# Four modulation pieces of a two-block model: scaled and added on ScalarE and GpSimd instead of streamed through TensorE

## What is computed

```python
cond = jax.nn.silu(c)
for i in range(DEPTH):                                  # DEPTH = 2
    mod = (cond @ ada_w[i] + ada_b[i])[:, None, :]      # 1024 -> 6 * 1024
    sh1, sc1, ga1, sh2, sc2, ga2 = jnp.split(mod, 6, axis=-1)
    u = x * (1 + sc1) + sh1
    ...                                                 # mixer
    x = _layer_norm(DEEPNORM_ALPHA * x + (1 + ga1) * y, ln_g[i, 0], ln_b[i, 0])
    u = x * (1 + sc2) + sh2
    ...                                                 # feed-forward
```

```python
def step(S, inp):
    r_t, k_t, v_t, w_t, a_t, b_t = inp
    sa = jnp.einsum('bhvk,bhk->bhv', S, a_t)
    S = S * w_t[:, :, None, :] + sa[..., None] * b_t[:, :, None, :] + v_t[..., None] * k_t[:, :, None, :]
    return S, jnp.einsum('bhvk,bhk->bhv', S, r_t)
```

## Time and profile before

| what | us |
|---|---|
| three executions | 2178.11, 2184.09, 2178.46 (median 2178.46) |
| the profiled execution | 2178.67 |
| its span | 2176.7 |
| TensorE busy | 2051.6 |
| VectorE busy | 1138.9 |
| ScalarE busy | 911.2 |
| GpSimd busy | 709.2 |

### The profile page before, as it was taken

The page is one execution under the profiler, slowest core; times in us unless marked ns, Lnnn a source line. Parts: engine busy times, 40 slices in busy tenths (PEclk is TensorE's granted clock), DMA queues, the critical chain, the costliest instruction groups (busy, mean ns, idle before and its releaser), DMA issues.

```text
span 2176.7 us, 40478 instructions
## 1 busy us (share of the span) xinstructions
PE 2051.6 (94%) x17526; PEld 1868.1 (86%) x17526; DVE 1138.9 (52%) x2177; ACT 911.2 (42%) x1331; POOL 709.2 (33%) x316
## 2 busy tenths in 40 slices
PE   3998999999999998999999999999999999999998
PEld 3786777889998887899999896799989998868897
DVE  6236645764483447654542447654264417357652
ACT  0452222544555425544333554333343336444443
POOL 0270000413683004136314560321561166313134
PEclk9998999999999999999999999999999999999999
DMA  8475334355443014554444440354445443314552
GB/s 323 190 294 222 128 134 150 142 188 194 155 173 138 3 40 155 190 181 154 176 174 175 153 157 22 126 174 175 170 146 175 175 174 136 136 48 151 190 194 78
DMA packets 49681, 340.48 MB, mean 156 GB/s; under 512 B 6368, under 2 KB 8416, under 8 KB 8672
## 3 DMA queue, kind: packets, MB, share of 16 engines
q1 hardware_dynamic: 49504, 337.90, 42.6%
HBM read 336.83 MB, written 1.05 MB: 155 GB/s over the span
## 4 chain that ended last, share of the span: by engine, by line
PE 84%; DVE 7%; ACT 3%; DMA 2%; issue 2%; POOL 1%; SPq 0%; ACTq 0%; POOLq 0%; DVEq 0%
PE bank L548 84%; DMA ada_ring<-ada 2%; POOL ring_low L2716 1%; PE bank L554 1%; DVE arena L2024 1%; DVE arena L2418 1%; DVE arena L2011 1%; DVE ZZ L2265 0%; DVE arena_parts L2047 0%; ACT high L1533 0%; DVE XX L2274 0%; DVE arena L2253 0%; POOL acc L2760 0%; ACT arena_parts L1558 0%; DVE acc L2117 0%
## 5 line engine op out<-in xcount | busy, mean ns | idle before, releaser
L548 PE MATMUL bank<-arena_parts,high 128*128 128x272 f32 (+2 forms) x4512 | 1019.2, 313 | 34.0 <-ACT arena_parts L1558 27.8
L548 PEld LDWEIGHTS bank<-arena_parts,high 128*128 128x128 f32 x4512 | 744.2, 190 | 83.6 <-issue 36.2
L548 PE MATMUL bank<-arena_parts,ring_low 128*128 128x272 f32 (+2 forms) x2736 | 778.6, 287 | 0.0
L1533 ACT ACTIVATE high<-ring 128x2048 fp32r<-128x2048 f32 x237 | 453.2, 1914 | 604.9 <-PE bank L548 589.4
L2716 POOL TENSOR_TENSOR ring_low<-ring,high 128x2048 fp32r<-128x2048 f32 x105 | 484.2, 4616 | 559.8 <-ACT high L1533 520.1
L548 PEld LDWEIGHTS bank<-arena_parts,ring_low 128*128 128x128 f32 (+1 forms) x2736 | 519.0, 190 | 1.2
L2060 DVE TENSOR_TENSOR ring_low<-ring,high 128x2048 fp32r<-128x2048 f32 x132 | 304.5, 2307 | 180.2 <-ACT high L1533 180.2
L548 PE MATMUL bank<-hidden_high,high 128*128 128x256 f32 (+1 forms) x1056 | 303.1, 287 | 0.0
L548 PE MATMUL bank<-hidden_low,high 128*128 128x256 f32 (+1 forms) x1056 | 301.0, 285 | 0.0
L548 PE MATMUL bank<-hidden_high,ring_low 128*128 128x256 f32 (+1 forms) x1056 | 300.2, 284 | 0.0
L2716 POOL TENSOR_TENSOR hidden_low<-arena,hidden_high 128x256 fp32r<-128x256 f32 (+1 forms) x132 | 111.7, 849 | 575.4 <-DVE hidden_high L2076 575.2
(11 more groups left out here) (332 smaller groups left out, 2160.5 us busy)
## 6 DMA issues: line engine op xcount, KB each, us to landing
ring<-stream SPq DMA_DIRECT2D x269, 1024.0 KB, 4.8
ada_ring<-ada SPq DMA_DIRECT2D x48, 1024.0 KB, 6.1
con<-consts SPq DMA_DIRECT2D x1, 1542.5 KB, 11.4
con<-consts SPq DMA_DIRECT2D x1, 1040.0 KB, 6.9
arena<-xin SPq DMA_DIRECT2D x1, 1024.0 KB, 11.5
out<-arena SPq DMA_DIRECT2D x2, 512.0 KB, 2.9
prob_even<-consts SPq DMA_DIRECT2D x1, 384.0 KB, 11.9
par<-params SPq DMA_DIRECT2D x1, 272.5 KB, 9.3
```

The source lines that it names most:

```text
L548: ins = nc.tensor.matmul(o, l, r, start=start, stop=stop_, skip_group_check=True)
L1533: act(high[:, q % HIGHS], ring[:, s % RING], ACT.Copy).then_inc(a.sig(high_ready), 1)
```

## The change

Pieces 6 to 9, those of the four iterations, are formed in the second way instead of the third. TensorE's loop issues no slab any more; behind step 5 it waits for `later_piece` and sums the partitions of `acc` with a column of ones (`sum_piece`), in bank 7 as before. ScalarE has, where `piece_rows` stood, eight scalings. GpSimd's additions are put into a function and run for pieces 6 to 9 as well, after it has seen that the four slabs of piece 5 (still TensorE's) were used. Pieces 5, 10 and 11 stay as they were, and so do SyncE's and VectorE's lists. What frees a slab of these pieces is the second of its two additions by GpSimd.

```diff
--- before.py
+++ after.py
@@ -1027,7 +1027,6 @@
                     grams(g, 2 * i + g)
                 for g in range(2):
                     turn_tokens(g, 2 * i + g)
-                slab = PIECE_SLABS * (FIRST + PROJECTION_PIECES + 1 + i)
                 for g in range(2):
                     turn_unit(g)
                 for l in range(1, 6):
@@ -1035,9 +1034,7 @@
                         middle(g, l)
                     for g in range(2):
                         merged(g, l)
-                    if l < 5:
-                        stream_slab(slab + l - 1)
-                sum_rows(FIRST + PROJECTION_PIECES + 1 + i)
+                sum_piece(FIRST + PROJECTION_PIECES + 1 + i, 7, later_piece)
                 for g in range(2):
                     eng.wait_ge(inverse_step[g], pe.nth(inverse_step[g]))
                 for g in range(2):
@@ -1690,7 +1687,8 @@
                     act(XR[:, g, :, :, 0], bank[g][:, 0:256].rearrange("p (e c f) -> p e c f", e=2, c=2), ACT.Copy).then_inc(a.sig(turned_ready[g]), 1)
                 if i == 0:
                     decay_powers(1)
-                piece_rows(FIRST + PROJECTION_PIECES + 1 + i)
+                for q in range(PIECE_SLABS):
+                    scaled(PIECE_SLABS * (FIRST + PROJECTION_PIECES + 1 + i) + q)
                 for g in range(2):
                     for tau in range(2):
                         b = FACTOR_BANKS[g][tau]
@@ -2749,7 +2747,8 @@
 
 
             eng.wait_ge(ada_used, FIRST * PIECE_SLABS)
-            for n in range(FIRST, FIRST + PROJECTION_PIECES):
+            def add_piece(n):
+
                 for k in range(DT):
                     a = PIECE_SLABS * n + k // 2
                     w_k = ada_ring[:, a % HIGHS, k % 2]
@@ -2761,6 +2760,12 @@
                 eng.wait_ge(*g.last)
                 ng.tensor_copy(acc[:, n % 2, 0:1], acc[:, n % 2, 0:1]).then_inc(later_piece, 1)
 
+            for n in range(FIRST, FIRST + PROJECTION_PIECES):
+                add_piece(n)
+            g.sent[ada_used] += PIECE_SLABS
+            eng.wait_ge(ada_used, PIECE_SLABS * (FIRST + PROJECTION_PIECES + 1))
+            for i in range(DT // 2):
+                add_piece(FIRST + PROJECTION_PIECES + 1 + i)
             eng.wait_ge(piece_summed, len(PIECES))
             base_sums(SEQ)
             for n in range(len(STAGES)):
```

## The result

The changed kernel took 2206.56 us, median of 3 runs (2202.37 to 2208.90), beside 2178.46 before: ratio 1.0125, 95% interval 1.0096 to 1.0154. It is 28.1 us slower. The forecast was 2197.4 us with a range up to 2204, so the measured time lies 9 us above the forecast and above the range: the sign and the main mechanism were right, and the term for the clock was too small. The profiled execution is the fastest of the three, 2202.37 us (span 2200.4), 23.7 us above the profiled one of before.

A forecast was written before the change was run, and what follows sets the result against it. TensorE, busy 94% of the span, was taken as the bound. Late closing products 7.0 + 3.5 + 0.8 and clock 7.4 make 18.7 us on the profiled 2178.67: 2197.4 us, range 2187 to 2204.

The forecast's parts named there:

- the sign and the main mechanism: Whole kernel: slower (chance 0.91), as TensorE newly waits for GpSimd's additions before the closing products.
- the clock's price: TensorE's clock falls to 0.50 behind waits: +3.4 us in iteration 0, nothing in 1, 2.0 each in 2 and 3.
- Bound and direction: Whole program: TensorE, busy 94% of the span, bounds it; an early delay moves everything behind it.
- What a slab is worth: Recurrence loop: each slab removed gives at most 0.88 us; four of sixteen are hidden, twelve give 10.6 us.
- The chain: From ScalarE's scalings through seven GpSimd additions to the closing products: 19.1 us; iterations 2 and 3 lose 0.8 together.
- Iteration 0: Scalings start behind two exponentials; TensorE waits 9.7 us, closing products start 7.0 us late, at 216.3.
- Iteration 1's first part: Loop up to the closing products: additions and VectorE's two-SBUF-input operations hold each other, +3.5 us (ends 0 and +6.2).
- its second part: Iteration 1 from the closing products on: TensorE's wait under 1 us, so no clock loss, 0 us.
- The first: Rival: the clock holds in iterations 2 and 3, 2193.4 us; chance 0.28.
- The second: Rival: additions hidden in the loop, chain no longer than 15.1 us, the whole 10.6 us gained, 2168.1 us; chance 0.05.
- The third: Rival: GpSimd also holds VectorE's loop operations out of PSUM, +11 us in each of four loops, 2230 us; chance 0.05.

The follow-up runs named there:

- the repeat: The changed kernel run once more, unedited: 2205.33 us, ratio 1.0113 to the kernel before.
- narrow_all: Changed kernel with scalings and additions of pieces 6 to 9 over 16 of 1024 columns, sums incomplete: 2179.95 us, ratio 0.9978 to before.
- narrow_piece_7: Changed kernel with GpSimd's additions over 16 of 1024 columns in iteration 1 alone, scalings at full width, sums incomplete: 2202.99 us, ratio 1.0082 to before.
- deferred_sum: Changed kernel with each piece's closing products and modulation one iteration later, the last behind the recurrence: 2186.14 us, ratio 1.0032 to before.
- scalings_first: Changed kernel with ScalarE's eight scalings ahead of the decay powers in iteration 0: 2200.12 us, ratio 1.0094 to before.
- deferred_but_7: Changed kernel with sums one iteration later and only pieces 6, 8 and 9 by GpSimd, piece 7 streamed through TensorE: 2177.94 us, ratio 0.9980 to before.
- deferred_but_7_again: Repeat of deferred_but_7, measured in another group: 2177.30 us, ratio 0.9975 to before.

## Why the prediction was right, and where not

**The step that failed is the clock's price.** The sum's other terms came out within 2.9 us together (14.2 for 11.3); this one was put at 7.4 us and measured 14.1, 11.6 in the repeat. In iteration 1 it was put at nothing, and 5.1 us were lost there, 2.6 in the repeat.

**Bound and direction: right.** TensorE's delays were not caught up: 25.06 us at the end of the recurrence, 23.7 at the end of the program.

**What a slab is worth: right in the step, not in the sum.** 0.88 us forecast, 0.87 measured. The forecast called three of the four slabs of iteration 1 free to remove. Without them the clock fell behind the loop (narrow_all and narrow_piece_7: iteration 1 2.8 and 2.9 us above before), where with them it was 1.00 at that place in four executions of five. In iterations 2 and 3 they are worth 3.3 and 3.5 us, forecast 3.5 each (deferred_sum).

**The chain: short by 0.8.** 19.1 us were forecast, 19.87 and 19.88 measured in iterations 2 and 3. Seven times the median of 2.36 leaves out what lies between two dependent additions; 17.35 us for seven is the number to use. It stood within reach: seven additions took 17.89 in the rows of before, and the 1.4 us above 16.5 were all put down to VectorE. With 17.35 as the base only some 0.5 us are left there for the two meetings. The chain is most of the 2.9 us by which the first parts were missed; 9.7 us (28.4 less 18.7) are missing in all.

**Iteration 0: right.** From the end of the second exponential (193.87) to the closing products it took 20.2 us, forecast 19.1; wait 10.40, forecast 9.7; loss 11.3 with the clock's part, forecast 10.4. scalings_first shows the cause: with the scalings ahead of it the wait was 2.08. In absolute time the forecast's 216.3 is 214.06, as everything began 3.3 us earlier and the chain was 1.1 longer.

**Iteration 1's first part: right, 3.9 for 3.5; its second part is where the clock's price failed first.** "Iteration 1 waits under 1 us: nothing" was the price there. The wait for GpSimd was 1.86 us, and 5.1 us were lost behind it (2.6 in the repeat). The forecast had VectorE's held operations in its sum as a delay (2.68 for 1.22, within the 2 to 3.5 forecast), but not that TensorE stands still while VectorE is held: 2.25 us, after which the clock fell at 246, inside the loop. deferred_sum has the same loss without any wait for GpSimd; narrow_piece_7, without hold and without wait, gets 6.1 of its 8.9 us back (3.7 against the repeat). The other 2.9 are a fall of the clock behind a loop without slabs.

**The clock's price: the term that was mis-sized.** 7.4 forecast (3.4, 0, 2.0, 2.0), 14.1 measured in the second parts (3.2, 5.1, 2.0, 3.9), 11.6 in the repeat (3.9, 2.6, 2.1, 3.0). The falls in iterations 2 and 3 were foreseen, 2.0 us each as an average over where the fall might be. They came early: the whole closing group ran at the low clock, 3.58 in place of 1.95, and the solve behind it too, up to 302 and 338 us. Iteration 2's 2.0 looks right and is not: before, the same part contained a stop of 1.48 us ("issue", at 284.44), so the fall cost some 3.5. Iteration 0's 3.2 has a stop of 0.98 before in it likewise, and iteration 1's 5.1 one of 0.42 in the changed kernel. So a fall cost 3.5 to 4.7 us in this execution and 1.9 to 4.0 in the repeat, where the forecast had nothing once, 2.0 twice and 3.4 once. How early a fall comes, and with it its price, differs between two executions of one kernel; that the first execution's falls came so early is in part chance.

**The rivals.** The first (the clock holds in iterations 2 and 3) is out: 0.50 in both. The second (the additions are hidden) is out: the seven additions alone took 17.35 us, where 15.1 was the limit for the whole chain; deferred_sum shows that even a version without the wait does not win, as long as all four pieces are moved. The third (GpSimd holds VectorE's operations out of PSUM) is out: 0.69 us as before. The Trainium skill's page SBUF — State Buffer (SBUF: two separate sides) describes the shared pair as an exclusive lock held for a whole instruction; the trace agrees: 1.46 us were added to VectorE's 1.22, and GpSimd's seven grew by twice 1.2.

**The range** ended at 2204. It allowed 3.4 us of clock in each of three iterations and none in iteration 1; what was lost there, 5.1 and 2.6 us, is what it lacked.

Not settled: why the clock falls earlier in one execution than in the next, whether iteration 1's slabs are what kept it up, and what the "issue" stops are. That the low clock is all of the second parts rests on the estimate above, half of the time at 0.50; no run kept the clock up throughout.

## What to carry to other kernels

A wait on TensorE costs more than its length: price each one with the low clock behind it (here some 2 to 5 us a fall), and look for the short stops inside a loop too, those of another engine's hold among them. Work that looks free to remove from TensorE may be what keeps its clock up; here that is likely and not shown. For a chain of dependent instructions take the measured length of a whole chain of the same kind, not count times median, and when a chain on a slow engine is about as long as its cover, take its result one iteration later: that gave 19 of 26 us back here.

## What the runs showed of the hardware that was not expected

- A stop of 2 us can be followed by the low clock: in deferred_sum TensorE stood still for 2.05 us up to 220.42 ("issue"), and from 222.0 to 225.7 the clock was 0.54. The length of the stop alone does not tell: later in the same run TensorE stood still for 2.97 us, and the clock stayed at 1.00 to the end of the iteration; and behind the same stop of 2.32 us it stayed at 1.00 in deferred_but_7 and was 0.50 from 222 to 224 in deferred_but_7_again. In scalings_first the closing products behind a wait of 2.08 us ran at full clock, and the clock fell right behind them.
- 8.33 us of matmuls of 400 columns did not protect the closing products behind a further 2.18 us of waiting: 3.57 us.
- Dependent GpSimd additions of 128x1024 start 2.5 us apart (17.35 us for seven), though each is 2.36 long.
- TensorE's stops without a visible cause came to 0.4 us in the changed kernel and 2.3 in its repeat, 2.5 before, and 3.7 to 7.1 in the seven executions of kernels that waited for GpSimd no more. In narrow_all they took 5.1 us out of the loops.
